# Six-row transfers for the second half of each expert's token rows in a mixture-of-experts kernel

## The chip, the cores and the metric

The kernel runs on 1 core of one Trainium2 chip. The metric is the device time of one execution in microseconds (us), the median over several runs. "Span" is the time from the first to the last instruction of one execution that was taken with the hardware profiler. PE is TensorE, DVE is VectorE, ACT is ScalarE, POOL is GpSimd, SP is SyncE, which here only issues DMA transfers. All data is 32-bit floating point.

## The reference

One inference step of a hybrid backbone, for 128 context tokens and 128 latent tokens with the same weights. Layer 0 is attention and a gated DeltaNet with a dense SwiGLU; layer 1 is a pooling mixer, then SwiGLU experts, two of eight for each token. The change touches only the experts:

```python
def _moe_swiglu(h, w_router, w_gate, w_up, w_down):
    logits = (h @ w_router).astype(jnp.float32)
    top_v, top_i = lax.top_k(logits, TOP_K)
    top_w = jax.nn.softmax(top_v, axis=-1)
    gates = jnp.sum(jax.nn.one_hot(top_i, N_EXP, ...) * top_w[..., None], axis=-2)
    out = jnp.zeros_like(h)
    for e in range(N_EXP):
        out = out + gates[..., e:e + 1] * _swiglu(h, w_gate[e], w_up[e], w_down[e])
    return out
```

`_swiglu` is `(silu(h @ wg) * (h @ wu)) @ wd`. A token has 1024 elements (4 KB), an expert's hidden width is 3584, so its three weight matrices have 44 MB together and the eight experts 352 MB.

## The kernel before, in words

The first part, to about 560 us, is layer 0, the mixer of layer 1 and the router. The router orders the experts by how many tokens each has, and GpSimd scatters the token rows into an area of DRAM, `rows_io`, with a region of 384 rows for each expert.

Then the experts are worked off at positions i = 0 to 7. Position i has room for `TOK * POS_G[i]` tokens, TOK = 32 and POS_G = (3, 2, 4, 2, 3, 3, 3, 2). At a position the weights are multiplied in stages: G0, U0 (gate and up, first part of the width), G1, U1 (second part), D0, D1 (down). A stage needs 4 units of weights (D1 needs 3); a unit is one DMA transfer of 1536 or 2048 KB into one of `RING` = 8 buffers (the names `ring_a`, `ring_b` and `raw` are where these buffers lie). All of them are issued by SP, in the order written in `pass_loads`: U0(i), D1(i-1), G1(i), then the row load for position i+1, D0(i), G0(i+1), U1(i). Before it issues a unit, SP waits until PE has finished with the buffer that the unit goes to.

The rows of position 0 are made on the chip. For i = 1 to 7, `row_load` (line 534) loads n = 32 * POS_G[i] rows of 4 KB from `rows_io` into `xrow`, a row to a partition: n is 64, 128, 64, 96, 96, 96 and 64. PE turns them (`turn_rows`, whose wait is on line 2375 and whose products are recorded at line 1837) into `hTf`, the operand of the gate and up products (line 2422). The down products are lines 2451 and 2456, with `ffT` or `xn` as operand. Unit loads are line 564 (the last unit is loaded in two halves, lines 558 and 559).

A DMA transfer raises its semaphore by 16 when all of it has landed. `xrow_loaded` counts the row loads, so PE waits for 16 times the number of transfers so far.

In what a program prints below, `pass_loads`, `row_load` and `moe_load` are SP's, `turn_rows` is PE's.

Of the kernel before, what the change touches and what calls it, by code (L numbers as in the profile page):

```python
# [43 lines left out]
N_EXP = 8  # L44
# [20 lines left out]
TOK = 32  # L65
POS_G = (3, 2, 4, 2, 3, 3, 3, 2)
# [3 lines left out]
REGION = 3 * P  # L70
# [34 lines left out]
def unit_at(i, phase, u):  # L105

    return UNIT_AT[i, phase, u]
# [13 lines left out]
for _n in range(PASS_UNITS):  # L121
    _, _ph, _u = UNITS[_n]
    COUNTED.append((COUNTED[-1] if COUNTED else 0) + (0 if _ph in PHASES and _u == 3 else 1))
PASS_COUNTED = COUNTED[-1]
STORES = tuple(4 if g == 2 else 8 for g in POS_G)
STORE_SUM = tuple(sum(STORES[:i]) for i in range(N_EXP + 1))
assert PASS_UNITS % RING == 0 and PASS_PARTS % 4 == 0 and len(UNITS) == PASS_UNITS
# [51 lines left out]
def build(nc, x_prompt, x_sample, cache_k, cache_v, state0, c, c_ctx, w_mod, b_mod, norm_g, final_g,  # L179
# [4 lines left out]
    with top:  # L184
        def sbuf(stack, name, shape, dt=F32):
            return stack.enter_context(nc.sbuf_tensor(name, [P, *shape], dt))

        s = {n: top.enter_context(nc.semaphore(n)) for n in SEMS}
        rows_io = nc.dram_tensor("rows_io", (N_EXP * REGION, D), F32, kind="Internal").ap()
# [111 lines left out]
        xrow = sbuf(tail, "xrow", [D])  # L301
# [147 lines left out]
        def _(sp):  # L449
# [77 lines left out]
            def row_load(p, i, e):  # L527

                if p == 0 and i == 1:
                    sp.wait_ge(s["rows_sent"], 64)  # L530
                sp.wait_ge(s["xg_turned"], N_EXP * p + i)
                n = TOK * POS_G[i]
                src = rows_io.rearrange("(e r) n -> e r n", r=REGION)[e, p * n:p * n + n]
                sp.dma_start(xrow[0:n, :], src).then_inc(s["xrow_loaded"], 16)

            def moe_load(p, n, src):

# [10 lines left out]
                else:  # L548
# [5 lines left out]
                    else:  # L554
                        sp.wait_ge(s["weights_used"], counted_base + PASS_COUNTED * q + COUNTED[m])
                dst = ring[k][:, 0:4 * D]
# [23 lines left out]
            def pass_loads(p):  # L580

                experts = [0]
                ff_loads(p, 0, "G0", 0)
                for i in range(N_EXP):
                    e = experts[i]
                    ff_loads(p, i, "U0", e)
                    if i:
                        down_loads(p, i - 1, 1, experts[i - 1])
                    ff_loads(p, i, "G1", e)
                    if i == 0 and p == 0:  # L590
                        sp.wait_ge(s["route_ready"], 2)
                    if i < N_EXP - 1:
                        r = POS_RANK[i + 1]
                        experts.append(nc.sync.value_load(order[0:1, r:r + 1], min_val=0, max_val=N_EXP - 1))
                        row_load(p, i + 1, experts[i + 1])
                    if i < N_EXP - 1:
                        down_loads(p, i, 0, e)
                        ff_loads(p, i + 1, "G0", experts[i + 1])
                    ff_loads(p, i, "U1", e)
                for c in range(2):  # L600
                    down_loads(p, N_EXP - 1, c, experts[N_EXP - 1])
# [236 lines left out]
        def _(act):  # L838
# [370 lines left out]
            def store_result(p, i, e):  # L1209

                act.wait_ge(s["weights_used"], counted_base + PASS_COUNTED * p + COUNTED[unit_at(i, "D1", 2)])
                act.wait_ge(s["rows_stored"], 16 * (STORE_SUM[N_EXP] * p + STORE_SUM[i] + 1))
# [619 lines left out]
        def _(pe):  # L1832
            MM = nc.tensor.matmul

            def turn(out, src, n=P):

                return nc.tensor.transpose(out, src, ident[0:n, 0:n])  # L1837
# [117 lines left out]
            for i, (kind, _) in enumerate(WIN_ORDER):  # L1955
# [3 lines left out]
                for h in range(2):  # L1959
                    n = 2 * i + h  # L1960
# [236 lines left out]
            for b in range(NB):  # L2197
                pe.wait_ge(s["vnew_saved"], 2 * b + 2)
                pe.wait_ge(s["attnT_saved"], b + 1)
                for h in range(H_B):  # L2200
                    for d in range(2):
                        i = 8 * b + 4 * d + h
# [35 lines left out]
            for h in range(2):  # L2238
                n = WOUT + h
# [132 lines left out]

            def turn_rows(p, i):

                pe.wait_ge(s["xrow_loaded"], 16 * ((N_EXP - 1) * p + i))
                pe.wait_ge(s["xg_hi"], N_EXP * p + i)
                for t in range(KT):
                    last = turn(ps[:, 6 + t // 4, (t % 4) * P:(t % 4 + 1) * P], xrow[:, t * P:t * P + P])
                last.then_inc(s["xg_turned"], 1)
# [86 lines left out]
            with pe.Fori(0, passes) as p:  # L2466
                pe.wait_ge(s["tokens_saved"], NB + 1 + p)
                product(p, 0, "G0")
                for i in range(N_EXP):
                    product(p, i, "U0")  # L2470
                    if i:
                        down_product(p, i - 1, 1)
                    product(p, i, "G1")
                    if i < N_EXP - 1:
                        turn_rows(p, i + 1)
                        down_product(p, i, 0)
                        pe.wait_ge(s["xg_hi"], N_EXP * p + i + 2)
                        product(p, i + 1, "G0")
                    else:
                        pe.wait_ge(s["late_sel"], 2 * NB)  # L2480
                        for v in range(2 * NB):
                            last = turn(ps[:, 6, v * P:v * P + P], late_row[:, v])
                        last.then_inc(s["late_turned"], 1)
                    product(p, i, "U1")
                gather(p + 1)
                for c in range(2):
                    down_product(p, N_EXP - 1, c)
# [44 lines left out]
```

## Time and profile before

| what | value |
|---|---|
| time, median of 3 runs | 1403.18 us (1402.5 to 1403.87) |
| the profiled execution | 1406.13 us, of which the span is 1404.4 us |
| granted TensorE clock, mean | 0.995 of full |
| PE busy | 1334.1 us (95% of the span) |
| DVE, ACT, POOL busy | 365.1, 282.9, 108.1 us |
| DMA | 500.15 MB in 103398 packets, mean 356 GB/s |

The profiled execution took 2.95 us longer than the median, and its span is 1.73 us shorter than its own time. In the rows further down, a DMA share is the mean busy share of the core's 16 DMA engines, and "idle before <- releaser" says how long an engine stood before an instruction and whose end it had waited for.

### The profile page before, as it was taken

To read this page: it belongs to the slowest core of one execution; us is meant where nothing else is said; L and a number is where in the kernel's file an instruction comes from. 1 tells how busy PE (TensorE), PEld (TensorE's weight loads), DVE (VectorE), ACT (ScalarE), POOL (GpSimd) and SP (SyncE) were. 2 spreads that over 40 slices of the span, in tenths; PEclk is the share of its full clock that TensorE was granted. 3 is DMA by queue.
4 is the path that set the end of the run, shared out by engine and by line. 5 is a ranking of instruction groups with operands and counts; after the bars stand their busy time and mean duration, and the time that the engine had idled before them with its cause. 6 is when DMAs were issued, how large, how long until landed. Compare 5 with 4: busy or idle time off the path is not lost.

```text
span 1404.4 us, 27801 instructions
## 1 busy us (share of the span) xinstructions
PE 1334.1 (95%) x12544; PEld 708.4 (50%) x12544; DVE 365.1 (26%) x453; ACT 282.9 (20%) x363; POOL 108.1 (8%) x182
## 2 busy tenths in 40 slices
PE   5999989999999999999999999999899999999876
PEld 2997776678888885333334433333233333333331
DVE  2857343655454454101000101000101101101103
ACT  2574534444433423000000000000000000000010
POOL 6200231323000001000000000000000000010010
PEclk9999999999999999999999999999999999999999
DMA  9854858899855568999999999999999999999995
GB/s 383 296 178 156 341 226 304 341 401 410 306 186 179 179 251 332 363 414 422 427 422 429 397 423 430 391 423 428 395 424 429 391 424 427 405 422 426 425 429 208
DMA packets 103398, 500.15 MB, mean 356 GB/s; under 512 B 10433, under 2 KB 14222, under 8 KB 74486
## 3 DMA queue, kind: packets, MB, share of 16 engines
q1 hardware_dynamic: 87376, 471.75, 83.7%
q10 hardware_dynamic: 13510, 18.29, 3.6%
q0 software_dynamic: 2400, 8.42, 1.6%
q8 instruction: 94, 1.54, 0.4%
q14 instruction: 18, 0.15, 0.0%
HBM read 478.74 MB, written 19.69 MB: 355 GB/s over the span
## 4 chain that ended last, share of the span: by engine, by line
PE 78%; DMA 17%; DVE 2%; ACT 1%; issue 1%; SPq 1%; ACTq 0%; DVEq 0%
PE ps L2422 30%; PE ps L2456 11%; DMA ring_a<-in_moe_down 7%; PE ps L439 6%; PE ps L441 6%; PE ps L440 6%; DMA ring_a<-in_moe_up 4%; PE ps L2451 3%; PE ps L1851 2%; DMA ring_a<-in_moe_gate 2%; DMA raw<-in_moe_down 2%; PE ps L1837 2%; PE ps L1983 1%; PE ps L1984 1%; PE ps L1985 1%; PE ps L1940 1%
## 5 line engine op out<-in xcount | busy, mean ns | idle before, releaser
L2422 PE MATMUL ps<-ring_a,hTf 128*32 128x512 f32 (+1 forms) x2160 | 208.8, 541 | 10.3 <-DMA ring_a<-in_moe_up 5.6
L2422 PE MATMUL ps<-raw,hTf 128*32 128x512 f32 (+1 forms) x2064 | 197.3, 538 | 1.2 <-DMA raw<-in_moe_up 1.2
L1793 DVE TENSOR_TENSOR hm<-gate_bc,ps 128x384 f32<-128x384 f32 (+1 forms) x30 | 17.9, 595 | 651.7 <-PE ps L2422 651.1
L380 DVE TENSOR_TENSOR w_lo<-raw,w_hi 128x2048 fp32r<-128x2048 f32 x60 | 147.6, 2464 | 119.4 <-ACT w_hi L376 119.4
L2422 PEld LDWEIGHTS ps<-ring_a,hTf 128*32 128x32 f32 x2160 | 70.3, 110 | 145.3 <-issue 127.6
L2422 PE MATMUL ps<-ring_b,hTf 128*32 128x384 f32 (+1 forms) x1408 | 138.4, 539 | 4.1 <-DMA ring_b<-in_moe_up 2.0
L376 ACT ACTIVATE w_hi<-raw 128x2048 fp32r<-128x2048 f32 x59 | 112.6, 1913 | 121.9 <-PE ps L441 103.3
L2422 PEld LDWEIGHTS ps<-raw,hTf 128*32 128x32 f32 x2064 | 70.9, 110 | 122.5 <-issue 118.8
L439 PE MATMUL ps<-w_hi,hTh 128*128 128x512 f32 x248 | 98.3, 396 | 1.5 <-DVE w_lo L380 1.5
L440 PE MATMUL ps<-w_hi,hTl 128*128 128x512 f32 x248 | 97.2, 392 | 0.0
L441 PE MATMUL ps<-w_lo,hTh 128*128 128x512 f32 x248 | 97.2, 392 | 0.0
L2422 PEld LDWEIGHTS ps<-ring_b,hTf 128*32 128x32 f32 x1408 | 46.9, 110 | 89.5 <-issue 82.4
L1214 ACT ACTIVATE yrow<-ps 128x768 f32<-128x768 f32 (+2 forms) x8 | 6.1, 758 | 378.0 <-PE ps L2451 196.9
L1207 ACT ACTIVATE gate_bc<-ps 128x384 f32<-128x384 f32 (+1 forms) x30 | 16.0, 534 | 211.4 <-PE ps L2422 211.4
L2456 PE MATMUL ps<-raw,ffT 128*32 128x512 f32 x448 | 54.6, 593 | 0.9 <-DMA raw<-in_moe_down 0.9
L825 POOL TENSOR_TENSOR rt<-rt,ones 128x4 f32<-128x4 f32 x1 | 0.2, 203 | 685.2 <-PE ps L1837 685.2
L439 PEld LDWEIGHTS ps<-w_hi,hTh 128*128 128x128 f32 x248 | 47.0, 189 | 11.5 <-DVE w_lo L380 1.8
L2456 PE MATMUL ps<-ring_a,ffT 128*32 128x512 f32 x416 | 48.8, 593 | 4.0 <-DMA ring_a<-in_moe_down 4.0
L441 PEld LDWEIGHTS ps<-w_lo,hTh 128*128 128x128 f32 x248 | 47.0, 189 | 9.9
L440 PEld LDWEIGHTS ps<-w_hi,hTl 128*128 128x128 f32 x248 | 46.9, 189 | 9.8 <-issue 0.2
L1851 PE MATMUL ps<-raw,vecs 128*32 128x512 f32 x384 | 47.4, 625 | 4.5 <-DMA raw<-in_w_mod 3.2
L2456 PE MATMUL ps<-ring_a,xn 128*32 128x512 f32 x320 | 39.7, 613 | 4.6 <-DMA ring_a<-in_moe_down 4.6
(422 smaller groups left out, 1530.4 us busy)
## 6 DMA issues: line engine op xcount, KB each, us to landing
raw<-in_w_mod SPq DMA_DIRECT2D x48, 1024.0 KB, 9.4
raw<-in_moe_down SPq DMA_DIRECT2D x22, 2048.0 KB, 29.3
ring_a<-in_moe_down SPq DMA_DIRECT2D x20, 2048.0 KB, 24.7
ring_a<-in_moe_up SPq DMA_DIRECT2D x14, 2048.0 KB, 27.2
raw<-in_moe_gate SPq DMA_DIRECT2D x13, 2048.0 KB, 25.5
ring_b<-in_moe_down SPq DMA_DIRECT2D x13, 2048.0 KB, 27.4
ring_a<-in_moe_gate SPq DMA_DIRECT2D x11, 2048.0 KB, 33.1
raw<-in_moe_up SPq DMA_DIRECT2D x10, 2048.0 KB, 17.6
```

The lines of the kernel that those rows point to most:

```text
L376: nc.scalar.activation(w_hi[:, w % SPLIT], raw[:, slot % RAW], ACT.Copy).then_inc(s["hi_ready"], 1)
L380: nc.vector.tensor_tensor(w_lo[:, w % SPLIT], raw[:, slot % RAW], w_hi[:, w % SPLIT].bitcast(F32), ALU.subtract).then_inc(s["lo_ready"], 1)
L439: nc.tensor.matmul(ps[:, bank, :], xh[:, kt0 + t, cut], w_hi[:, k % SPLIT, t, :], start=st, stop=False)
L440: nc.tensor.matmul(ps[:, bank, :], xl[:, kt0 + t, cut], w_hi[:, k % SPLIT, t, :], start=False, stop=False)
L441: last = nc.tensor.matmul(ps[:, bank, :], xh[:, kt0 + t, cut], w_lo[:, k % SPLIT, t, :], start=False, stop=en)
L1207: nc.scalar.activation(sgm[at % SILUS][:, 0:w], ps[:, part % 4, 0:w], ACT.Silu).then_inc(s["silu_ready"], 1)
L1793: VT(hm[:, g, 0:w], sgm[at % SILUS][:, 0:w], ps[:, part % 4, 0:w], ALU.mult).then_inc(s["h_ready"], 1)
L1837: return nc.tensor.transpose(out, src, ident[0:n, 0:n])
L1851: last = MM(ps[32 * j:32 * j + 32, bank, :], cstat[:, kt, :], raw[:, n % RAW, j, :], start=kt == 0, stop=kt == MOD_KT - 1)
L2422: last = MM(ps[TOK * j:TOK * j + TOK, part % 4, 0:w], hTf1[:, kt, q * P + TOK * g:q * P + TOK * g + TOK], wt[:, kt % 2, j, :], start=kt == ...
L2451: last = MM(ps[TOK * k:TOK * k + TOK, 5, 0:256], ffT[c][:, g, cut], wt[:, 256 * k:256 * k + 256], start=st, stop=en)
L2456: last = MM(ps[TOK * k:TOK * k + TOK, 4 + g // 2, :], ffT[c][:, g, cut], wt[:, 512 * h:512 * h + 512], start=st, stop=en)
```

## The change

The load of an expert's rows is cut into pieces. The first half of the rows goes in one transfer (32, 64 or 48 rows, shared by all sixteen engines, as before the whole was), the second half in transfers of six rows and one of the remainder. So 64 rows are 1 + 5 + 1 transfers, 128 rows 1 + 10 + 1, 96 rows 1 + 8; all seven loads together are 60 transfers where they were 7. PE waits for the sum of them.

```diff
+def row_pieces(n):
+
+    cuts = [0, *range(n // 2, n, ROWS), n]
+    return list(zip(cuts, cuts[1:]))
+
+
+ROWS = 6
+LOADS = (0, *(len(row_pieces(TOK * g)) for g in POS_G[1:]))
+LOAD_SUM = tuple(sum(LOADS[:i + 1]) for i in range(N_EXP))
...
                 n = TOK * POS_G[i]
-                src = rows_io.rearrange("(e r) n -> e r n", r=REGION)[e, p * n:p * n + n]
-                sp.dma_start(xrow[0:n, :], src).then_inc(s["xrow_loaded"], 16)
+                rows_e = rows_io.rearrange("(e r) n -> e r n", r=REGION)
+                for a, b in row_pieces(n):
+                    sp.dma_start(xrow[a:b, :], rows_e[e, p * n + a:p * n + b]).then_inc(s["xrow_loaded"], 16)
...
-                pe.wait_ge(s["xrow_loaded"], 16 * ((N_EXP - 1) * p + i))
+                pe.wait_ge(s["xrow_loaded"], 16 * (LOAD_SUM[N_EXP - 1] * p + LOAD_SUM[i]))
```

In the order of SP's instructions before the change, the first row load (i = 1, 64 rows) stands between the wait for the router's result and the four units of D0. An ISA row is a wait or an address step.

```order
L594 TENSOR_LOAD order
L594 ISA x2
L534 ISA
L534 DMA xrow<-rows_io 64x1024
L564 DMA ring_a<-in_moe_down 128x4096 x3
L564 DMA ring_b<-in_moe_down 128x4096
```

The same place of the changed kernel, where the lines of this code have moved by 12:

```order
L606 TENSOR_LOAD order
L606 ISA x2
L546 ISA
L546 DMA xrow<-rows_io 32x1024
L546 ISA
L546 DMA xrow<-rows_io 6x1024
L546 ISA
L546 DMA xrow<-rows_io 6x1024
...
L546 ISA
L546 DMA xrow<-rows_io 2x1024
L576 DMA ring_a<-in_moe_down 128x4096 x3
L576 DMA ring_b<-in_moe_down 128x4096
```

Between the fences one transfer has become seven, each with its address step, and the weight units behind it are the same in the same order; three more pairs of rows with `6x1024` are left out.

On PE nothing moves. Before the change the turn of the rows stands between the last G1 product and the first D0 product of the position before:

```order
L2422 MATMUL ps<-ring_b,hTf 32x384 x23
L2375 ISA
L1837 MATMUL ps<-ident,xrow 128x128 [waits xg_hi,xrow_loaded]
L1837 MATMUL ps<-ident,xrow 128x128 x7
L2433 REGISTER_ALU
L2456 MATMUL ps<-ring_a,ffT 32x512 [waits ring0,y_saved,ff_turned]
```

The changed kernel has the same rows there with lines 12 higher (2387, 1849, 2434, 2445, 2468); the wait on `xrow_loaded` is for 16 x 7 in place of 16 at i = 1.

## Rows read from the trace of the kernel before

**Rows 1.** The page: 40 slices of the span, busy share in tenths
```profile
PE   5999989999999999999999999999899999999876
...
DMA  9854858899855568999999999999999999999995
```

**Rows 2.** The page: the chain that ended last, shares by engine
```profile
PE 78%; DMA 17%; DVE 2%; ACT 1%; issue 1%; SPq 1%; ACTq 0%; DVEq 0%
```

**Rows 3.** Waits of PE from 540 us: us in total, times, longest us
```profile
PE ps L2456 <- DMA ring_a<-in_moe_down: 8.6, 6, 2.5
PE ps L2422 <- DMA ring_a<-in_moe_up: 5.6, 5, 1.5
```

**Rows 4.** Chain that ended last, from 1200 us: start us, us, what
```profile
1278.83 31.11 DMA ring_a<-in_moe_down
...
1346.37 38.89 DMA ring_a<-in_moe_down
```

**Rows 5.** PE by time: start us, us, engine line op xcount [idle before <-releaser]
```profile
1270.98 7.67 PE L2422 MATMUL ps<-ring_a,hTf 128*32 128x512 f32 x80 [1.75 <-DMA ring_a<-in_moe_gate]
...
1367.21 3.64 PE L2456 MATMUL ps<-ring_b,ffT 128*32 128x512 f32 x32 [3.18 <-DMA ring_b<-in_moe_down]
1373.28 3.64 PE L2456 MATMUL ps<-ring_a,ffT 128*32 128x512 f32 x32 [2.43 <-DMA ring_a<-in_moe_down]
1379.44 5.13 PE L2456 MATMUL ps<-ring_a,xn 128*32 128x512 f32 x32 [2.52 <-DMA ring_a<-in_moe_down]
1385.31 3.64 PE L2456 MATMUL ps<-ring_a,xn 128*32 128x512 f32 x32 [0.73 <-DMA ring_a<-in_moe_down]
```

**Rows 6.** A stretch of 60 us: busy of each engine, PEclk, DMA share, GB/s
```profile
1320.00:1380.00 60.00, 46.70 (x500) 18.83 (x496) 7.11 (x8) 4.86 (x8) 4.03 (x5) 0.99 1.00 421
```

**Rows 7.** Stretches at the end, with the same columns
```profile
1370.00:1376.00 6.00, 3.57 (x36) 0.92 (x32) 3.32 (x4) 0.00 (x0) 0.00 (x0) 1.00 0.98 415
1376.00:1378.00 2.00, 0.92 (x12) 0.01 (x2) 1.17 (x1) 0.00 (x0) 0.00 (x0) 1.00 0.96 406
1378.00:1380.00 2.00, 0.56 (x4) 0.23 (x8) 0.00 (x0) 0.00 (x0) 0.00 (x0) 0.77 0.70 297
1380.00:1384.00 4.00, 4.00 (x32) 1.08 (x24) 0.00 (x0) 0.00 (x0) 0.00 (x0) 0.69 0.50 212
1384.00:1388.00 4.00, 3.27 (x36) 0.90 (x32) 3.27 (x4) 0.00 (x0) 0.00 (x0) 1.00 0.50 211
1388.00:1390.00 2.00, 2.00 (x24) 0.56 (x20) 1.22 (x1) 0.00 (x0) 0.00 (x0) 1.00 0.16 61
```

**Rows 8.** Line 559 (last weight transfer): duration ns, start us; landing
```profile
L559 SPq DMA_DIRECT2D ring_b<-in_moe_down x1: 333/333/333, 1350.2 to 1350.2; - x1
...
DMA to landing us min/median/max: 39.9/39.9/39.9
```

**Rows 9.** DMA queue of instruction fetches, 560 to 1352 us: packets, MB, share
```profile
q8 instruction: 65, 1.06, 0.5%
```

**Rows 10.** Line 534 (row loads): duration ns min/median/max, first and last start
```profile
L534 SPq DMA_DIRECT2D xrow<-rows_io x7: 346/554/7839, 570.0 to 1202.3; - x7
...
DMA to landing us min/median/max: 10.1/22.9/32.5
```

**Rows 11.** Line 564 (weight loads): us from issue to landing
```profile
DMA to landing us min/median/max: 7.7/27.0/38.9
```

**Rows 12.** Waits of SP's queue: us in total, times, longest us
```profile
SPq L564 <- PE ps L2422: 434.5, 119, 27.9
```

**Rows 13.** SP's queue by time, at two of the row loads: start us, us
```profile
981.85 7.84 SPq L534 DMA_DIRECT2D xrow<-rows_io  x1
...
1202.35 6.86 SPq L534 DMA_DIRECT2D xrow<-rows_io  x1
```

**Rows 14.** Line 534 at 981.85 us alone: us from issue to landing
```profile
DMA to landing us min/median/max: 32.5/32.5/32.5
```

**Rows 15.** PE by time, where it turns the rows of i = 5
```profile
1017.24 1.09 PE L1837 MATMUL ps<-ident,xrow 128*128 128x128 f32 x8
```

## The prediction

> **What bounds the kernel now.** I read the page first. TensorE is busy in nearly every slice, and the DMA engines are at nine tenths in all the second half [rows 1]. The chain that ended last counts 78% of the span for PE and 17% for DMA [rows 2]. Both are close to full, so the stage decides. The change lives between 570 us and 1230 us, in the expert layer, and I asked there for what PE waited on: from 540 us on it waited some 30 us in all, nearly all of it for weight units that were landing (8.6 and 5.6 us are the two greatest sums), and never for `xrow` [rows 3]. The last chain says the same: from 1237 us to the end its long pieces are DMA transfers, such as 31.1 us and 38.9 us, with short PE pieces between [rows 4]. In the list of PE's work by time almost every unit from 1270.98 us on starts on a landing (1.75 us of wait there; 3.18, 2.43, 2.52 and 0.73 us before the last four that waited) [rows 5]. The DMA share is 1.00 from 1320 to 1380 us, at 421 GB/s [rows 6]. So what sets the end is the rate at which units land. Behind the last landing stand fixed steps: the last products, the final turn and norm, and the store.
>
> **What a landing is made of.** A unit of 2048 KB is spread over 16 DMA engines and counts as landed when the slowest has done its part. The stretches around the end show how unequal they are: the share is 0.98 to 1376 us, 0.96 to 1378, 0.70 to 1380, then 0.50 with 212 and 211 GB/s to 1388 us, and 0.16 to 1390 us [rows 7]. The last transfer was issued at 1350.2 us and landed 39.9 us later, at 1390.1 us [rows 8]. A share of 0.50 for eight microseconds is eight engines that have nothing left and eight that still work, each at 211 / 8 = 26.4 GB/s. The early eight were done at about 1379 us, the late eight at 1388 to 1390 us: the late ones are some 9 to 11 us behind. The idle time by the end is 6 x 0.02 + 2 x 0.04 + 2 x 0.30 + 4 x 0.50 + 4 x 0.50 + 2 x 0.84 = 6.5 us as a mean over 16 engines, which is what a perfect share would gain, and no more. The lag fits the instruction fetches: 65 packets with 1.06 MB take 0.5% of 16 engines over 792 us [rows 9], which is 63 us of one engine, or 8 us each if they fall on eight.
>
> **What the change adds and removes.** No byte is added. The rows are 64 + 128 + 64 + 96 + 96 + 96 + 64 = 608, of 4 KB each. Before, each engine carries 608 / 16 = 38. After, the first halves give each 19. The second halves go in 49 transfers of six rows and four remainders (2, 4, 2 and 2 rows). A transfer of six whole rows can use six engines at most; I take it that it uses six, and always the same: then two of them get 49 + 4 = 53 rows of the second halves, two 50 and two 49, so +34, +31 and +30 against before, and the ten others get 19 fewer (10 x 19 = 2 x 34 + 2 x 31 + 2 x 30). A row costs its engine 4096 B / 26.4 GB/s = 0.155 us at the rate of [rows 7]. So ten engines are relieved by 19 x 0.155 = 2.9 us each and six loaded by 4.6 to 5.3 us.
>
> What that does to the end depends on whether a late engine is among the six, and no row names engines. If all eight late ones are among the ten, they are done 2.9 us sooner, and the six loaded ones, which had 9 to 11 us in hand, still have 4 us or more against the old end. The relief passes to PE: its last four waits in [rows 5] add up to 8.9 us, so PE can take 2.9 us. The units' landings move earlier bit by bit from the second expert on, since the lag is one sum over the layer.
>
> The costs. **SP** issues 53 more transfers. A row load took 0.346 us of issue at the least and 0.554 us in the median [rows 10]: 18 to 29 us for 53, at most 11 x 0.554 = 6.1 us in one expert (i = 2); the address step that the order shows ahead of each has no row here and is small beside it. The backlog hides it: SP's weight loads were issued 7.7 us (least) and 27.0 us (median) before landing [rows 11], and SP itself stood 434.5 us waiting for PE to free buffers [rows 12], so it catches up before the next expert. Two row issues took 6.9 and 7.8 us [rows 13]: SP there was held by full queues, and smaller transfers wait for the same space. If that cover were gone, 6.1 us per expert less what was in hand would appear. I take 0. **PE** keeps its order; only the count it waits for changes. Rows were in place early: at i = 5 the load was issued at 981.9 us and landed 32.5 us later, at 1014.4 us, and PE turned it at 1017.24 us, without a wait for it [rows 13 to 15]. That margin is 2.8 us. There an engine of the six would carry 3 + 8 = 11 rows for 6, 5 x 0.155 = 0.8 us more, plus part of the 8 x 0.5 = 4 us of later issues, which overlap with the queue of 30 us ahead. If it were late, one stall of 1 to 2 us of PE, which DMA uses to get ahead; taken as 0. **The DMA engines** themselves may spend time on each small transfer. No row shows a six-row transfer. The bounds: 0, and one row's time each (0.155 us), 53 x 0.155 = 8.2 us on the six engines. The nearest row is the row load itself, whose packets flow in a full queue (share 1.00 in [rows 6]), so near 0. Either bound falls on the six alone, and the ten feel nothing of it, so it is 0 on the end as long as the six have their 9 to 11 us in hand.
>
> **The skill's rules.** The Trainium skill, in DMA: Bandwidth & Descriptors, section "Why a DMA increments its semaphore by 16 and not by 1", says that a transfer from this queue is split over the largest number up to 16 that divides its rows, on the lowest-numbered engines. By this rule six rows would always load the same six; no row of before shows it. The same page, section "Rules for kernel authors", speaks against the change: under 64 KB a transfer is mostly overhead, and these are 24 KB. By the page's fixed part of about 2.0 us for one, an estimate is 53 x 2.0 = 106 us if they stood one behind another; that is the rival with overhead, below, at its worst.
>
> **The sum.** 0 (PE) + 0 (SP) + 0 (the six) - 2.9 (the ten) = -2.9 us. The profiled execution would go from 1406.13 us (span 1404.4) to 1403.2 us. It lies 2.95 us above the median of the runs, so against 1403.18 us I predict 1400.3 us. A measurement here tells about 0.2% (2.8 us) from no change, so this is just at that bound.
>
> **Rivals.** (B) **A late engine is among the six.** The lag then grows by 4.6 to 5.3 us instead of shrinking, and units land later by as much: 1403.18 + 4.6 = 1407.8, up to 1408.5 us. It decides as soon as one late engine is loaded, or, with overhead, when 5.3 us and the overhead on the six exceed the 9 to 11 us in hand; at the full 8.2 us that is 13.5 us, and the end moves by +2.5 to +4.5 us. For it: [rows 7] gives the number of late engines, not their place, and if every second one were late three would be among the six. Against it: late engines that form one half of the numbers at the upper end escape altogether. I judge the upper half likelier than the rest together, by choice, not by a row. 0.24. (C) **The relief is lost.** The six-row transfers move round the engines or are cut finer, so that no tilt arises; or the fetches' place follows the load; or the rows cost late engines less than 0.155 us each. Time 1403.2 us, from 1401.8 to 1404.8. 0.19. (D) **Small transfers have a price on SP or in the queue**: a unit issued 3.8 (11 x 0.346) to 6.1 us later than now lands late. It would be seen as a starved queue, for which a lead under 6.1 us would be needed; the least lead is 7.7 us [rows 11]. If it came out at half in one or two experts, +3 to +6 us, about 1407.5 us. 0.05. The forecast, (A), has 0.52, with a range of its own of 1399.2 to 1402.2 us (a relief of 1 us, where the lead is shared with other causes, to 4 us, with a row at 0.21 us).
>
> **Chances and range.** Faster by over 0.2% (below 1400.4 us): two thirds of A and the lower edge of C, 0.38, since nothing in the rows makes a row cheaper than 0.155 us on a late engine and contention may make it dearer. Within 0.2%: the rest of A and most of C, 0.36. Slower: B, most of D, 0.26. The range reaches from 1399.2 us to 1407.9 us: it leaves out the upper part of B and D and the lower edge of A, together 2 in 10.
>
> **What would show it.** Right: the stretches at the end have 0.50 for less than eight microseconds, and the last landing comes 2 to 3 us sooner against the rest; waits of PE for landings shrink by 2 to 3 us; none for `xrow` appears. B: those waits grow by 4 to 5 us and the time at a half or less lengthens, with the share falling in more steps. C: the same shares as now. D: SP's issues come later, and the share falls under 1.00 near a row load. I am wrong above all if the late engines lie among the six, or if a small transfer costs its engine as much as a row.

## The result, and the profile after

The change made the kernel slower: 1406.35 us median of 20 runs (1403.46 to 1410.68) against 1403.64 us of 20 runs of before; ratio 1.0023, 95% interval 1.0016 to 1.003, that is +3.2 us (2.2 to 4.2). I had forecast 1400.3 us, a relief of 2.9 us. The time lies in the stated range, but on the other side of no change: it is rival B. One execution of all those below ran at a granted clock of 0.752 and took 1735.41 us (e12); the ratios leave it out.

The profiled execution took 1409.74 us with a span of 1408.0 us, 3.6 us more than before. The last weight transfer shows where they are. Of the source view of the changed kernel, its line (571) with issue and landing:

```profile
L571 SPq DMA_DIRECT2D ring_b<-in_moe_down x1: 332/332/332, 1354.5 to 1354.5; - x1
...
DMA to landing us min/median/max: 39.2/39.2/39.2
```

It landed at 1354.5 + 39.2 = 1393.7 us, against 1390.1 us in [rows 8]. What follows it is as long as before (1408.0 - 1393.7 = 14.3 us, and 1404.4 - 1390.1 = 14.3 us). So all 3.6 us lie in how late the weights land. The stretches at the end, with the columns of [rows 7]:

```profile
1376.00:1380.00 4.00, 3.22 (x32) 0.94 (x32) 3.40 (x4) 0.00 (x0) 0.00 (x0) 1.00 0.94 396
1380.00:1384.00 4.00, 1.44 (x16) 0.34 (x12) 1.08 (x1) 0.00 (x0) 0.00 (x0) 1.00 0.77 323
1384.00:1388.00 4.00, 2.97 (x28) 0.79 (x20) 0.93 (x2) 0.00 (x0) 0.00 (x0) 1.00 0.38 159
1388.00:1390.00 2.00, 1.12 (x12) 0.42 (x16) 1.97 (x2) 0.00 (x0) 0.00 (x0) 1.00 0.05 20
1390.00:1392.00 2.00, 2.00 (x24) 0.61 (x20) 1.59 (x2) 0.00 (x0) 0.00 (x0) 1.00 0.10 37
1392.00:1394.00 2.00, 2.00 (x24) 0.55 (x20) 0.00 (x0) 0.00 (x0) 0.00 (x0) 1.00 0.04 16
```

Before, the share stood at 0.50 for eight microseconds and then ended: eight late engines, close together. Now it falls through 0.77 and 0.38, and from 1388 us on it is 0.05, 0.10 and 0.04, with 20, 37 and 16 GB/s. One engine of sixteen is a share of 0.06 and some 26 GB/s. A stretch cut to the middle of this shows it without rounding:

```profile
1388.00:1391.00 3.00, 2.12 (x20) 0.68 (x24) 2.93 (x3) 0.00 (x0) 0.00 (x0) 1.00 0.06 25
```

So for more than five microseconds what was left was the work of a single engine, and the last units wait for it. (The 0.10 holds one packet more, an instruction fetch of 16 KB; the list of DMA queues for 1390 to 1393 us has eleven packets of the weights' queue and that one.) Fifteen engines were done by about 1388 us, two microseconds sooner than the last of before: the relief happened, and one engine was too late to give it to anyone.

PE shows a longer wait, and once a lower clock. PE by time at i = 5; first a row of before, the unit that comes two ahead of the turn in [rows 15]:

```profile
1008.43 4.08 PE L2422 MATMUL ps<-ring_a,hTf 128*32 128x384 f32 x48 [0.95 <-DMA ring_a<-in_moe_gate]
```

and then the same unit and what follows it, of the changed kernel:

```profile
1009.59 5.77 PE L2434 MATMUL ps<-ring_a,hTf 128*32 128x384 f32 x48 [2.26 <-DMA ring_a<-in_moe_gate]
1015.18 4.05 PE L2434 MATMUL ps<-ring_b,hTf 128*32 128x384 f32 x48
1019.16 1.09 PE L1849 MATMUL ps<-ident,xrow 128*128 128x128 f32 x8
```

and the stretches around it:

```profile
1006.00:1010.00 4.00, 1.74 (x28) 0.48 (x20) 0.00 (x0) 0.00 (x0) 0.00 (x0) 1.00 1.07 325
1010.00:1014.00 4.00, 4.00 (x36) 1.38 (x32) 0.00 (x0) 0.00 (x0) 0.00 (x0) 0.57 1.01 386
```

PE stood 2.26 us for one gate unit; the granted clock fell to 0.57 in the next stretch, so most of it at 1.2 GHz in place of 2.4, and the 48 products took 5.77 us, where before they took 4.08 after a wait of 0.95 us. The rows of i = 5 are turned at 1019.16 us in place of 1017.24, with no wait for `xrow` (the turn follows its neighbour at once). The waits of PE from 540 us on, with the rows that answer to [rows 3]:

```profile
PE ps L2468 <- DMA ring_a<-in_moe_down: 9.3, 6, 2.6
PE ps L2434 <- DMA ring_a<-in_moe_gate: 5.8, 4, 2.3
PE ps L2434 <- DMA ring_a<-in_moe_up: 5.2, 5, 1.5
```

The sums are hardly greater than before: all waits for landings from 540 us on come to 29.8 us, after 29.7. PE's busy time in that part grew by 3.1 us (829.5 after 826.4), of which the slow stretch above is 1.7 us (5.77 - 4.08); the rest I did not trace. Over the whole span it is 1338.3 us after 1334.1, but that holds another stretch of lower clock, at 166 to 171 us (0.66, where before had 1.00), ahead of the experts; e1 has it too, and it cannot be the change's. Nor is a lower clock a mark of the change: its twenty executions have a mean granted clock of 0.993, and so have the 92 of the kernel before beside the experiments. In the chain of shares the DMA part has grown from 17% to 19% and SP's from 1% to 3%:

```profile
PE 74%; DMA 19%; SPq 3%; DVE 2%; ACT 1%; issue 1%; ACTq 0%; DVEq 0%
```

SP had its part of the change too. Its queue by time at i = 5, where one row load took 7.84 us in [rows 13]:

```profile
984.51 12.20 SPq L546 DMA_DIRECT2D xrow<-rows_io  x9
996.82 4.13 SPq L576 DMA_DIRECT2D raw<-in_moe_down  x3
```

The traces also tell how many engines a small transfer uses, since they hold every step in which a DMA raised a semaphore. For `xrow_loaded` these are 112 before (7 x 16). After the change they are 469: 112 for the seven first pieces, 304 for the 304 rows of the small ones, and one more for each of the 53. So a transfer of six rows is raised in six steps and one for the rest of the 16, where one of 32 rows takes sixteen: it is the work of six engines, as the prediction took it. e2 below (fives) has 404 = 112 + 240 + 52, e11 (sevens) 462 = 112 + 304 + 46.

Two theories follow from this. **T**: an engine that was late already is among the six, the number of transfers costs nothing. **S**: the transfers themselves cost, on SP (12.20 us against 7.84 here) or in the queues, and the single late engine is a by-product.

### The profile page after: what moved, and what is told of

Its sections match the earlier page's. It is cut to its first block, busy times and chain, and to the rows that moved or that the text cites. A ratio compares the mean times of both kernels' runs of the same rounds, so it can differ in the third digit from the quotient of the medians.

```text
span 1408.0 us, 27960 instructions
## 1 busy us (share of the span) xinstructions
PE 1338.3 (95%) x12544; PEld 718.3 (51%) x12544; DVE 361.3 (26%) x453; ACT 282.7 (20%) x363; POOL 107.6 (8%) x182
## 4 chain that ended last, share of the span: by engine, by line
PE 74%; DMA 19%; SPq 3%; DVE 2%; ACT 1%; issue 1%; ACTq 0%; DVEq 0%
PE ps L2434 28%; PE ps L2468 10%; DMA ring_a<-in_moe_up 6%; PE ps L450 6%; PE ps L451 6%; PE ps L452 6%; DMA ring_a<-in_moe_down 4%; PE ps L1863 2%; DMA ring_a<-in_moe_gate 2%; DMA raw<-in_moe_down 2%; PE ps L2463 2%; PE ps L1849 2%; SPq L546 2%; DMA ring_b<-in_moe_down 2%; SPq L576 1%; PE ps L1995 1%
## 5 line engine op out<-in xcount | busy, mean ns | idle before, releaser
L391 DVE TENSOR_TENSOR w_lo<-raw,w_hi 128x2048 fp32r<-128x2048 f32 x60 | 143.8, 2401 | 122.6 <-ACT w_hi L387 122.6
L2434 PEld LDWEIGHTS ps<-ring_a,hTf 128*32 128x32 f32 x2160 | 73.3, 110 | 145.3 <-issue 126.1
```

The source lines that it names most:

```text
L391: nc.vector.tensor_tensor(w_lo[:, w % SPLIT], raw[:, slot % RAW], w_hi[:, w % SPLIT].bitcast(F32), ALU.subtract).then_inc(s["lo_ready"], 1)
L2434: last = MM(ps[TOK * j:TOK * j + TOK, part % 4, 0:w], hTf1[:, kt, q * P + TOK * g:q * P + TOK * g + TOK], wt[:, kt % 2, j, :], start=kt == ...
```

## The experiments

All were timed against the kernel before on the same chip: e1 to e4 on one, e5 to e8 on a second, e9 to e12 on a third. In e1 to e8, e11 and e12 only the cuts of `row_pieces` and the size differ from the changed kernel; all rows are loaded in each. What the cuts make of the engines' rows, in a table: "others" are the engines that get only the transfers of 16 rows or more. The columns are worked out from the cuts, with the low-numbered engines taking the pieces. The traces name no engine; "the sixth" is the one that a piece of six rows reaches and a piece of five does not.

| kernel | transfers | sixth engine, rows against before | others | ratio (95%) |
|---|---|---|---|---|
| the change | 60 | +30 | -19 | 1.0023 (1.0016 to 1.003) |
| e1 sixteens | 38 | 0 | 0 | 0.9996 (0.9984 to 1.0007) |
| e2 fives | 59 | -15 | -15 | 0.9984 (0.9971 to 0.9996) |
| e12 fives, again | 59 | -15 | -15 | 0.9979 (0.9966 to 0.9991) |
| e3 fours | 51 | -11 | -11 | 0.9984 (0.9972 to 0.9995) |
| e4 threes | 49 | -7 | -7 | 1.0007 (0.9999 to 1.0016) |
| e5 sixes, the rows of e2 | 48 | +23 | -15 | 1.0037 (1.0024 to 1.005) |
| e6 fives, half of the rows | 71 | -19 | -19 | 0.9989 (0.9975 to 1.0003) |
| e7 sixes, all rows | 103 | +61 | -38 | 1.0065 (1.0051 to 1.0079) |
| e8 fours, half of the rows | 83 | -19 | -19 | 0.9999 (0.9986 to 1.0011) |
| e9 before, and 35 x 5 rows | 42 | 0 | 0 | 0.9992 (0.9981 to 1.0003) |
| e10 before, and 35 x 6 rows | 42 | +35 | 0 | 1.0018 (1.0007 to 1.0029) |
| e11 sevens, half of the rows | 53 | +23 | -19 | 1.0025 (1.0013 to 1.0037) |

**e1: all rows in sixteens.** Every engine has its 38 rows as before, in 38 transfers.

```diff
-    cuts = [0, *range(n // 2, n, ROWS), n]
+    cuts = [0, *range({64: 0, 96: 0, 128: 0}[n], n, ROWS), n]
+    cuts = sorted(set(cuts))
...
-ROWS = 6
+ROWS = 16
```

> All rows in transfers of sixteen rows: 38 transfers in place of 7 (the change has 60), every engine with 38 rows as before. Theory T (one engine that was already late is among the six that got the second halves; number of transfers costs nothing): the time of before, ratio 0.999 to 1.001, share of 0.50 for some eight microseconds before the last landing, as before. Rival S (small transfers cost time on SP or in the queues): 31 of 53 extra transfers, so about six tenths of the change's 2.7 to 3.6 us, ratio near 1.0013, the lag of the late engines as before.

Measured 1403.73 us, ratio 0.9996. Its stretches before the last landing are those of before, with the same 0.50:

```profile
1380.00:1384.00 4.00, 3.64 (x32) 1.13 (x32) 0.00 (x0) 0.00 (x0) 0.00 (x0) 1.00 0.55 231
1384.00:1388.00 4.00, 1.77 (x20) 0.58 (x24) 2.39 (x3) 0.00 (x0) 0.00 (x0) 1.00 0.50 210
```

The extra 31 transfers cost nothing that is measured. The upper end of the interval, 1.0007, lies below the 1.0013 of S.

**e2 and e12: five rows for six.** To have about the same load on each low engine as in the change, the pieces begin at row 48 of 64, 48 of 96 and 80 of 128.

```diff
-    cuts = [0, *range(n // 2, n, ROWS), n]
+    cuts = [0, *range({64: 48, 96: 48, 128: 80}[n], n, ROWS), n]
+    cuts = sorted(set(cuts))
...
-ROWS = 6
+ROWS = 5
```

> The last 16 rows of 64, 48 of 96 and 48 of 128 in transfers of five rows (and the remainder): 57 to 60 transfers, five engines get about 30 rows more and the others 15 fewer. Theory T, if the late engine is the sixth of the six: all eight late engines are relieved by 15 x 0.155 to 0.2 = 2.3 to 3 us and the time falls by as much, ratio 0.998. Theory T, if it is one of the first five: as the change, ratio 1.002 to 1.003, and a share of 0.06 (one engine of sixteen) for several microseconds before the last landing. Rival S: the same number of transfers as the change, so 1.002, without the single late engine.

> e2_five once more, on the chip of the runs beside it, to narrow its interval: theory T 0.998 to 0.999; rival S 1.002.

Measured 1401.17 us (0.9984) and 1401.77 us (0.9979): faster, with 59 transfers. No engine stands alone at the end of e2; more than eight work nearly to the last:

```profile
1380.00:1384.00 4.00, 4.00 (x28) 1.07 (x24) 0.00 (x0) 0.00 (x0) 0.00 (x0) 0.69 0.80 339
1384.00:1388.00 4.00, 3.38 (x36) 0.94 (x32) 3.35 (x4) 0.00 (x0) 0.00 (x0) 1.00 0.69 293
1388.00:1390.00 2.00, 2.00 (x27) 0.52 (x16) 1.14 (x1) 0.00 (x0) 0.00 (x0) 1.00 0.17 66
```

The share is 0.80 and 0.69 where it was 0.50 and 0.50 in [rows 7]: the five that were early have taken over work from the late ones. This profiled execution was a long one of its kernel (1406.05 us against a median of 1401.17), so its shares are read here and not its end. For the end there is e12, with 1403.26 us. Its last unit landed at 1387.3 us, 2.8 us sooner than in [rows 8], and its shares have moved with it:

```profile
1380.00:1384.00 4.00, 3.54 (x36) 0.95 (x32) 2.42 (x3) 0.00 (x0) 0.00 (x0) 1.00 0.69 292
1384.00:1388.00 4.00, 4.00 (x40) 1.17 (x36) 2.07 (x2) 0.00 (x0) 0.00 (x0) 1.00 0.14 57
```

The same traces answer S where it took its number from. SP spent as long on the rows of i = 5 in e2, a faster kernel, as in the change (12.20 us), and 12.66 us in e12:

```profile
981.66 12.84 SPq L547 DMA_DIRECT2D xrow<-rows_io  x11
```

In the chain that ended last SP's share is 0% in e2 and 1% in e12.

**e3 and e4: four rows and three.** e3, and then e4:

```diff
-    cuts = [0, *range(n // 2, n, ROWS), n]
+    cuts = [0, *range({64: 48, 96: 64, 128: 96}[n], n, ROWS), n]
+    cuts = sorted(set(cuts))
...
-ROWS = 6
+ROWS = 4
```

```diff
-    cuts = [0, *range(n // 2, n, ROWS), n]
+    cuts = [0, *range({64: 48, 96: 80, 128: 112}[n], n, ROWS), n]
+    cuts = sorted(set(cuts))
...
-ROWS = 6
+ROWS = 3
```

> The last 16 rows of 64, 32 of 96 and 32 of 128 in transfers of four rows: 44 small transfers and 7 others, four engines get 33 rows more, the others 11 fewer. Theory T: if the late engine is not among these four, the late ones are relieved by 11 rows, 1.7 to 2.2 us, ratio 0.9985, no single straggler; if it is, ratio 1.002 to 1.003 with a share of 0.06 before the last landing. Rival S: 44 extra transfers, about 1.0015 to 1.002 in either case.

> The last 16 rows of each load in transfers of three rows and one: 42 small transfers, three engines get 28 rows more (one of them 35), the others 7 fewer. Theory T: if the late engine is not among these three, ratio 0.999 (7 rows, 1.1 to 1.4 us of relief); if it is, 1.002 to 1.003 with the single straggler. Rival S: about 1.0015 to 1.002 in either case.

e3 came out at 1401.58 us, 0.9984, as T has it for four early engines. e4 missed: 1.0007 (0.9999 to 1.0016) where T had 0.999. It is neither the straggler's 1.002 nor the forecast relief of 1.1 us. Its interval leaves 0.999 out, so this is a miss of T beyond the noise of these runs, and what ate the relief is open.

**e5: six rows for five, with the rows of e2.** The minimal pair: against e2 only `ROWS = 6`. The two ran on different chips, so they are compared by their ratios to the kernel before.

```diff
-ROWS = 5
+ROWS = 6
```

> The same rows as in e2_five (the last 16 of 64, 48 of 96 and 48 of 128) but in transfers of six: the only difference to e2_five is that the sixth engine gets 38 of these rows and the five others fewer. Theory T, with the late engine as the sixth: the late one gets 38 - 15 = 23 rows more, 3.6 to 4.6 us, and its trace shows one engine alone behind; ratio 1.002 to 1.003, against 0.9984 of e2_five. Rival (any engine of the low ones will do, it is the amount that counts): as e2_five or better, 0.998.

Measured 1408.4 us, 1.0037, more than the 1.002 to 1.003 expected: with eleven transfers fewer than e2 it is 0.5% slower, and the single engine is back (the 0.11 again holds an instruction fetch):

```profile
1384.00:1388.00 4.00, 3.13 (x32) 1.12 (x32) 0.00 (x0) 0.00 (x0) 0.00 (x0) 1.00 0.57 238
1388.00:1390.00 2.00, 0.51 (x8) 0.00 (x0) 1.39 (x2) 0.00 (x0) 0.00 (x0) 1.00 0.20 86
1390.00:1392.00 2.00, 1.57 (x16) 0.55 (x20) 1.93 (x3) 0.00 (x0) 0.00 (x0) 1.00 0.11 37
1392.00:1394.00 2.00, 2.00 (x24) 0.63 (x20) 1.17 (x1) 0.00 (x0) 0.00 (x0) 1.00 0.06 25
```

Together, e2 and e5 decide between the theories: fewer transfers, slower, and what differs is which engines they use. They also name the engine: five are harmless and six are not, so it is the sixth, if six rows use the engines of five and one more (e9 and e10 ask that again, on one chip).

**e6: the change with 5 for 6.**

```diff
-ROWS = 6
+ROWS = 5
```

> The change with 5 in place of 6: the second half of the rows in transfers of five. Theory T: all late engines are relieved by 19 rows (2.9 to 4 us), ratio 0.9972 to 0.998; the five early engines get about +40 rows (6 to 8 us) and come close to the late ones, so that the share at the end falls later and more steeply than before. If the early engines have less in hand than that, 0.998 to 1.000. Rival S (number of transfers): 1.002, since there are more of them than in the change.

Measured 1400.68 us, but 0.9989 (0.9975 to 1.0003): the lower median, with an interval that reaches no change. It undoes the loss of the change (its interval lies below the change's), and is not told apart from e2.

**e7: all rows in sixes.**

```diff
-    cuts = [0, *range(n // 2, n, ROWS), n]
+    cuts = [0, *range({64: 0, 96: 0, 128: 0}[n], n, ROWS), n]
+    cuts = sorted(set(cuts))
```

> All rows in transfers of six: 104 transfers, six engines with +63 rows, ten with 38 fewer. Theory T: twice the change's load on the one late engine, ratio 1.004 to 1.006, the single engine twice as far behind the others (12 to 14 us before the last landing with a share near 0.06 to 0.3). Rival S: 97 extra transfers for 53, ratio 1.004, but without that lag.

(The cuts make 103 transfers, one fewer than I wrote.) Measured 1412.03 us, 1.0065, a little over the 1.006 expected, +9.1 us for 61 rows more on the sixth, which is 0.149 us a row beside the 0.155 us of the prediction. Its stretches from the point where the many are done:

```profile
1382.00:1384.00 2.00, 1.50 (x16) 0.26 (x8) 1.40 (x2) 0.00 (x0) 0.00 (x0) 1.00 0.83 346
1384.00:1386.00 2.00, 0.00 (x0) 0.00 (x0) 0.00 (x0) 0.00 (x0) 0.00 (x0) 1.00 0.48 199
1386.00:1388.00 2.00, 1.93 (x20) 0.81 (x24) 0.00 (x0) 0.00 (x0) 0.00 (x0) 1.00 0.12 49
1388.00:1390.00 2.00, 1.71 (x16) 0.32 (x8) 0.22 (x1) 0.00 (x0) 0.00 (x0) 1.00 0.09 39
...
1392.00:1394.00 2.00, 2.00 (x24) 0.65 (x20) 1.97 (x2) 0.00 (x0) 0.00 (x0) 1.00 0.10 37
1394.00:1396.00 2.00, 2.00 (x24) 0.58 (x20) 0.37 (x1) 0.00 (x0) 0.00 (x0) 1.00 0.06 25
```

The long tail of one or two engines' share starts at 1386 us and lasts ten microseconds, the last six of them with one engine (0.06, or a little more where other queues have packets). The change's lasted some six. It is longer, as T has it, but short of the twelve to fourteen expected.

**e8: half of the rows in fours.**

```diff
-ROWS = 6
+ROWS = 4
```

> The second half in transfers of four: 76 small transfers; four engines get 76 - 19 = 57 rows more, the others 19 fewer. Theory T: the late engines are relieved by 2.9 to 4 us, but the four get 57 x 0.155 to 0.235 = 8.8 to 13.4 us with 9 to 11 us (and the 3 to 4 of the relief) in hand against the old end, so they set the end themselves at the upper price: ratio 0.998 to 1.002, with four engines (a share of 0.25) at the end at the upper price. Rival S: 1.003 to 1.004.

Measured 1402.93 us, 0.9999: the relief of 19 rows is gone again, with four engines at +57 rows. It lies in the expected span between the two prices of a row. A share of 0.25 at the end did not show, and the finer stretches say why:

```profile
1384.00:1386.00 2.00, 1.72 (x20) 0.42 (x16) 1.91 (x2) 0.00 (x0) 0.00 (x0) 1.00 0.76 320
1386.00:1387.00 1.00, 1.00 (x14) 0.27 (x10) 0.96 (x2) 0.00 (x0) 0.00 (x0) 1.00 0.72 303
```

Twelve engines of sixteen (0.75) worked to nearly 1387 us, where it was eight before: the eight late ones and four more, which with 57 rows each had used up their lead. That these four also took the relief fits the trace, but this profiled execution was 2.7 us above its median, so it is not shown.

**e9 and e10: extra transfers beside untouched row loads.** They copy rows of an input to an unused area of DRAM and compute nothing. This is e10; e9 has 5 for 6 (in the rows, not in the five transfers), and SP's last wait counts the 35 more.

```diff
                 sp.dma_start(xrow[0:n, :], src).then_inc(s["xrow_loaded"], 16)
+                if p == 0:
+                    for m in range(5 * i - 5, 5 * i):
+                        sp.dma_start(extra[6 * m:6 * m + 6, 0:D],
+                                     x_prompt[0].rearrange("(a b) n -> a b n", b=2)[0:6, 0, :]).then_inc(s["y_stored"], 16)
```

> The kernel before, its row loads untouched, with five extra transfers of five rows behind each row load (35 in all, from an input to an unused area of DRAM; an addition that computes nothing). Theory T: each of the first five engines carries 35 rows more (5.4 us at 0.155 us, more if a copy within DRAM costs more), none of them late, so the time of before, ratio 0.999 to 1.001. Rival S (small transfers, or extra bytes as such): 35 extra transfers, 1.0015.

> As e9, but each extra transfer has six rows: the same number of transfers, with one engine more that is loaded, the sixth, by 35 rows. Theory T: the sixth is late, so the end moves by 35 x 0.155 = 5.4 us less up to 2 us that it may have in hand against the latest, ratio 1.0025 to 1.004. Rival S: as e9.

Measured 0.9992 (1402.83 us) and 1.0018 (1406.71 us), the latter under the 1.0025 to 1.004 expected. The two intervals do not meet. The extra transfers raise `y_stored` in 35 x 6 and 35 x 7 steps, five and six engines and one for the rest. Here nothing is relieved, bytes and transfers are added in both, and `xrow` is left alone, so where the rows land in it plays no part; 35 rows on each of five engines are free, and one row more for each transfer, on the sixth, costs 0.26% or 3.6 us. Two rows of each kernel, first e9, then e10, show the end of the many and the rest:

```profile
1382.00:1384.00 2.00, 2.00 (x24) 0.56 (x20) 1.97 (x2) 0.00 (x0) 0.00 (x0) 1.00 0.37 152
1384.00:1386.00 2.00, 2.00 (x24) 0.60 (x20) 0.25 (x1) 0.00 (x0) 0.00 (x0) 1.00 0.05 20
```

```profile
1386.00:1388.00 2.00, 1.37 (x16) 0.48 (x20) 1.97 (x2) 0.00 (x0) 0.00 (x0) 1.00 0.15 57
1388.00:1390.00 2.00, 2.00 (x24) 0.59 (x20) 1.34 (x2) 0.00 (x0) 0.00 (x0) 1.00 0.07 29
```

e9 falls from 0.37 to 0.05; e10 has a stretch at one engine's share before its last landing.

**e11: seven rows.**

```diff
-ROWS = 6
+ROWS = 7
```

> The change with 7 in place of 6: seven engines get 43 to 50 rows of the second halves, +24 to +31 against before. Theory T: the sixth is among them, so 24 x 0.155 to 0.2 = 3.7 to 4.8 us, ratio 1.002 to 1.0035. Rival (transfers of six are special): near 1.000 or 0.998, as for five and four.

(The cuts give the seven 39 to 46 rows, +20 to +27, and the sixth +23.) Measured 1408.29 us, 1.0025. Transfers of six are not special; those that reach the sixth engine are. The share stays near two engines (0.125) at the end, where it stayed at one after the change (an instruction fetch stands in the second row):

```profile
1387.50:1389.00 1.50, 1.50 (x16) 0.47 (x20) 1.47 (x2) 0.00 (x0) 0.00 (x0) 1.00 0.13 55
1388.00:1390.00 2.00, 2.00 (x24) 0.53 (x18) 1.93 (x3) 0.00 (x0) 0.00 (x0) 1.00 0.16 61
1390.00:1392.00 2.00, 2.00 (x24) 0.65 (x20) 0.54 (x1) 0.00 (x0) 0.00 (x0) 1.00 0.11 45
```

Two engines alone, at 55 GB/s, to about 1391.5 us: the seventh is late as well. The change and e7 loaded the first five with more rows than this, and there one engine stood alone.

## Why the prediction was wrong, step by step

**What bounds: right.** The end is set by landings of weight units, and a landing by the slowest engine. All kernels move the same weights, and who carries the rows made them differ, from 0.9979 to 1.0065.

**The count of rows and their price: right.** +34, +31 and +30 rows for six, -19 for ten; 0.149 us a row in e7 for the 0.155 us taken. Over the five kernels that load the sixth engine the price is (3.2 + 5.2 + 9.1 + 2.5 + 3.5) / (30 + 23 + 61 + 35 + 23) = 23.5 / 172 = 0.137 us, with single values from 0.07 (e10) to 0.23 (e5). The intervals of these two, 0.03 to 0.12 and 0.15 to 0.31 us, do not meet, so one price does not fit all five; what lies between them is open. (A lead of the sixth against the latest engine would lower a value, and the kernels ran on different chips.)

**Whether a late engine is among the six: the step that failed.** The prediction said "I judge the upper half likelier than the rest together, by choice, not by a row". The runs say: the first five low-numbered engines are early and the sixth is late (e2 with e5, e9 with e10). So the term of -2.9 us of the sum was never paid out; in its place the sixth engine alone set the end. Rival B named this mechanism, its deciding point (one late engine) and +4.6 to +5.3 us; measured are +3.2 us (2.2 to 4.2), less than its term, of which the two microseconds by which late engines differ among themselves in [rows 7] may be a part.

By the rule of the Trainium skill, DMA: Bandwidth & Descriptors, section "Why a DMA increments its semaphore by 16 and not by 1", which the prediction cites, six rows go to the lowest-numbered six engines, five to the lowest five, so that e5 contains e2 and one engine more. The runs agree in the count (one step of the semaphore for each row of a small transfer) and in always the same engines (one alone at the end after 35 and more transfers of six; fives 0.9984, sixes 1.0037). That they are the lowest-numbered no trace shows.

**The relief of the late engines: right where the sixth is left out and few rows are moved, given to nobody in the change.** With the sixth left out, 15 rows less on the late ones (2.3 us at 0.155 us) gave -2.2 and -2.9 us (e2, e12), and 11 rows less (1.7 us) gave -2.2 us (e3). Beyond that it does not follow the term: 19 rows less (2.9 us) gave -1.5 us in e6, not clear of no change, and nothing in e8, where the loaded engines had used up their lead; 7 rows less gave nothing in e4.

**SP, PE and the transfers at 0: right for SP and the count, right for `xrow`.** SP did spend 12.20 us on nine row transfers where one took 7.84, and e1, e2 and e9, with 12.84 us in e2, show that it costs nothing measurable. The same page's rule that transfers under 64 KB are mostly overhead, section "Rules for kernel authors", does not decide here: 59 transfers, most of 20 KB, made the kernel faster. The estimate of 106 us took the page's fixed part of 2.0 us, which it states for transfers issued by GpSimd; against it stand +3.2 us for 53 more transfers of SP's, and e2, with 52 more, was faster.

**What I had not counted** is a lower clock behind a longer wait: once, 5.77 us for 48 products in place of 4.08. As the end is set by landings, and the mean granted clock of the runs is the same, no run shows that it adds to the time.

**What stays open.** Which others than the sixth and the seventh are late; why these engines are late (the instruction fetches of [rows 9] have the right amount, 8 us each for eight, but no run moved them); the miss of e4; why e5 and e10 differ in the price of a row; and whether e6 is better than e2.

The version that beats both kernels is e2: 0.9984 and 0.9979 in two measurements.

## What to carry to other kernels

Where every large transfer is spread over all engines and the work waits for its slowest part, look at the DMA share just before the last landing: a share that stands at a half for microseconds says that small transfers can be had for nothing on the engines that are early, as long as their lead lasts (57 rows each used it up in e8), and cost time on those that are late. Small transfers choose their engines by their number of rows, so 5 and 6 rows can differ in sign. Before such a tilt is built, a few extra transfers of k rows beside the real work (e9, e10) tell which k reaches a late engine.

## What the runs showed of the hardware

- One row more in each small transfer decided its effect: 35 extra transfers of five rows 0.9992, of six rows 1.0018.
- A transfer of fewer than eight rows was the work of as many engines as it had rows: `xrow_loaded` was raised in 416 + 53 steps by the change's 60 transfers, 16 for each large one, one for each row of a small one, and one for the rest of each.
- One DMA engine, the sixth that a small transfer uses, was behind in every kernel that loaded it (the change, e5, e7, e10, e11), and the seventh with it in e11. Alone at the end it moved 25 GB/s (e5, share 0.06).
- A wait of 2.26 us was followed by a granted clock of 0.57 in the next four microseconds; the wait of 0.95 us at the same place before was not (48 products in 4.08 us).
